# Streaming encoder step on one core: rows of v four steps behind rows of u, and another order of the first loads

## The reference, cut to what matters

```python
z = jnp.einsum('bld,de->ble', hn, w_in)            # hn = RMSNorm(x), projections of all tiles
...
def block(xb):                                     # 128 tokens
    qh = jnp.einsum('td,de->te', xb, w_q)...
    s = jnp.einsum('thcd,hcnd->thcn', qh, sub_keys)
    ...                                            # top 16 of 8 heads: eidx (128, 8, 16), gates g
    act = gelu(jnp.einsum('td,thkd->thk', xb, u_tab[eidx]))
    return jnp.einsum('thk,thkd->td', g * act, v_tab[eidx])
```

## Time and profile before

| | |
|---|---|
| median of 3 runs | 3998.46 us (3996.53 to 4018.43) |
| the profiled execution | 4045.73 us |
| its span, first to last instruction | 4044.0 us |
| busy: PE, DVE, POOL, ACT | 2780.5, 2535.5, 2261.6, 1054.3 us |
| moved by DMA | 1389.41 MB, mean 344 GB/s |
| queue of the indirect DMAs | 1215.35 MB, 79.9% of 16 engines' span |
| first rows of u issued | 312.87 us |
| first boundary (`turn_weights`) | 723.49 us |
| second boundary | 1110.24 us |
| last boundary | 3842.26 us |

### The profile page before, as it was taken

One profiled execution on the slowest core, in us unless ns is written; L12 is line 12 of the kernel. 1 busy time (PEld: TensorE's weight loads), 2 busy tenths in 40 slices (PEclk: granted clock), 3 DMA queues, 4 the chain that ended last, 5 costly groups with the idle time before them and its releaser, 6 DMA issues.

```text
span 4044.0 us, 48466 instructions
## 1 busy us (share of the span) xinstructions
PE 2780.5 (69%) x16300; PEld 1405.1 (35%) x16300; DVE 2535.5 (63%) x6869; ACT 1054.3 (26%) x2881; POOL 2261.6 (56%) x2365
## 2 busy tenths in 40 slices
PE   7999999677577747774777488658774674333365
PEld 6845644333234314441443144224331331000021
DVE  2445657775876678758776787687767556544400
ACT  3312212323232223222322323233322111110121
POOL 1102443666666666656666666665656666666665
PEclk9999999778677867776778687868875575555567
DMA  7645798999999999999999999999999999999998
GB/s 204 187 142 163 259 344 272 375 374 389 375 373 363 388 371 378 372 365 358 359 375 372 366 366 376 387 376 351 384 360 357 373 391 351 368 369 365 366 362 314
DMA packets 545781, 1389.41 MB, mean 344 GB/s; under 512 B 61289, under 2 KB 225313, under 8 KB 545537
## 3 DMA queue, kind: packets, MB, share of 16 engines
q0 software_dynamic: 335024, 1215.35, 79.9%
q1 hardware_dynamic: 198288, 161.34, 12.5%
q10 hardware_dynamic: 12224, 9.63, 0.9%
HBM read 1352.93 MB, written 33.04 MB: 343 GB/s over the span
## 4 chain that ended last, share of the span: by engine, by line
PE 16%; POOL 11%; DMA 11%; DVE 11%; issue 8%; another core or an unknown queue 5%; ACT 1%; DVEq 0%; ACTq 0%; POOLq 0%
POOL d_vb L1726 6%; DMA d_ub<-in_peer_u_dram,d_eid 5%; PE d_pY L1756 5%; POOL d_ub L1707 5%; DMA d_vb<-in_peer_v_dram,d_eidT 5%; DVE d_ub L1920 5%; PE d_pS L855 2%; PE r_pB L1456 2%; PE d_pS L941 1%; PE d_pS L921 1%; PE d_pS L880 1%; POOL d_ub L1726 1%; PE r_pB L1471 1%; PE d_pS L869 1%
## 5 line engine op out<-in xcount | busy, mean ns | idle before, releaser
L1920 DVE CUSTOM_DVE_ANT_0 d_ub<-d_ub,d_pX 128x1024 f32<-128x1024 f32 x1024 | 1242.5, 1218 | 645.9 <-DMA d_ub<-in_peer_u_dram,d_eid 515.9
L1707 POOL DMA_INDIRECT d_ub<-in_peer_u_dram,d_eid x1152 | 1135.6, 986 | 868.8 <-DVE d_hdot L1920 379.7
L1756 PE MATMUL d_pY<-d_vb,d_dg 128*32 128x256 f32 x8768 | 958.6, 515 | 851.2 <-DMA d_vb<-in_peer_v_dram,d_eidT 547.7
L1726 POOL DMA_INDIRECT d_vb<-in_peer_v_dram,d_eidT x1096 | 1043.2, 952 | 768.0 <-PE d_pY L1756 260.0
L1756 PEld LDWEIGHTS d_pY<-d_vb,d_dg 128*32 128x32 f32 x8768 | 256.2, 127 | 1459.1 <-issue 1273.7
L1795 ACT ACTIVATE d_dg<-c_late_sb,d_wgtT 128x32 f32<-128x32 f32 x1152 | 333.8, 314 | 1259.8 <-PE d_pY L1756 675.2
L707 PE MATMUL d_pX<-d_wq,d_vb 128*128 128x512 f32 (+3 forms) x1536 | 475.2, 462 | 17.8 <-DMA d_vb<-in_w_in_dram 9.7
L707 PEld LDWEIGHTS d_pX<-d_wq,d_vb 128*128 128x128 f32 x1536 | 271.9, 201 | 184.1 <-issue 117.5
L1456 PE MATMUL r_pB<-r_side,c_small_sb 128*128 128x128 f32 (+15 forms) x1152 | 175.7, 319 | 20.1 <-issue 14.0
L1920 DVE CUSTOM_DVE_ANT_0 d_ub<-d_ub,d_vb 128x1024 f32<-128x1024 f32 x128 | 155.2, 1220 | 49.6 <-DMA d_ub<-in_peer_u_dram,d_eid 46.4
L1456 PEld LDWEIGHTS r_pB<-r_side,c_small_sb 128*128 128x128 f32 x1152 | 174.7, 241 | 33.3 <-issue 23.7
(11 more groups left out here) (282 smaller groups left out, 3544.8 us busy)
## 6 DMA issues: line engine op xcount, KB each, us to landing
d_vb<-in_w_in_dram SPq DMA_DIRECT2D x68, 512.0 KB
d_ub<-in_peer_u_dram,d_eid POOLq DMA_INDIRECT x1152
d_vb<-in_peer_v_dram,d_eidT POOLq DMA_INDIRECT x1096
r_side<-in_cache_k_dram SPq DMA_DIRECT2D x16, 1024.0 KB
r_side<-in_cache_v_dram SPq DMA_DIRECT2D x16, 1024.0 KB
d_wo<-in_w_out_dram SPq DMA_DIRECT2D x6, 2048.0 KB, 9.4
d_wo<-in_peer_w_q_dram SPq DMA_DIRECT2D x4, 2048.0 KB, 8.9
scratch_h<-t_shared SPq DMA_DIRECT2D x9, 512.0 KB
```

The lines of the kernel that those rows point to most:

```text
L1707: pool.indirect_dma_start(out=ub[:, g % R, :], out_offset=None, in_=io["peer_u"][0], in_offset=off).then_inc(u_in[g % R], 16)
L1726: pool.indirect_dma_start(out=to, out_offset=None, in_=io["peer_v"][0], in_offset=off).then_inc(landed, 16)
L1756: m = nc.tensor.matmul(pY[q * QT:(q + 1) * QT, g % 2, :], dg[:, n % DG, :], rows[:, q * QD:(q + 1) * QD], start=k % QT == 0, stop=k % QT = ...
L1920: nc.vector.tensor_tensor_reduce(out=ub[:, g % R, :], in0=ub[:, g % R, :], in1=xflat if i else xn_of(0), scale=1.0, scalar=0.0, op0=ALU.mu ...
```

## The change

There are two parts.

**Rows of v four steps behind.** `LAG = 4`. The rows of v for expert `k` of tile `i - 1` are fetched and weighed in step `k + 4` of period `i`. `turn_weights` moves from step 0 to step 2, the copy of the weights and the first columns to step 3, `weigh` to step 1, the residuals, the last norm and the store by four steps. On ScalarE `copy_x` stands before `gelu`. TensorE's wait for `wT_done` moves from the start of a mixer to its first transposes.

**The beginning.** ScalarE issues x of the first tile and nothing else, and does one root of a constant before it waits. The eight small loads are issued by GpSimd, behind x of the second tile. The bias vector, the exponentials and the constants of the recurrence move from behind the first chunks to `pos[7]` to `pos[10]`, the eighth to the eleventh chunk, x of the third tile and the sub-keys behind the sixth segment (`p_acc` 6), `gfs` and `g2` behind x of the sixth tile, and the near blocks and keys by three chunks.

```diff
             load_x(1)
+            pool.dma_start(rb_, io["rel_bias"]).then_inc(c_t_in, 16)
...
+                pool.dma_start(lq[:, n, :], io[name].partition_broadcast(P)).then_inc(c_t_in, 16)
+            pool.wait_ge(p_acc, 6)
+            load_x(2)
...
             yield -320
-            act.dma_start(rb_, io["rel_bias"]).then_inc(c_t_in, 16)
...
+            act.dma_start(nx[:, 0, :], rows_of(io, "x", NORMS[0])).then_inc(p_first, 16)
             act.wait_ge(c_eps, 1)
-            act.wait_ge(p_first, 32)
+            nc.scalar.activation(nst[:, 3:4], eps[:], ACT.Sqrt)
+            act.wait_ge(p_first, 48)
...
-            at.append((-285, 3, exps, ()))
+            at.append((pos[8] + 0.9, 3, exps, ()))
...
+        LAG = 4
...
-                for i in range(NT + 1):
-                    for k in range(NEXP):
+                for i in range(NT + 2):
+                    for k in range(NEXP if i <= NT else LAG):
...
-                        if i:
-                            n = NEXP * (i - 1) + k
+                        n = NEXP * (i - 1) + k - LAG
+                        if n >= 0:
...
-                        if 1 <= i <= NT:
-                            if k == 0:
-                                turn_weights(i - 1)
-                            weigh_rows(i - 1, k)
+                        if 1 <= i <= NT and k == 2:
+                            turn_weights(i - 1)
+                        n = NEXP * (i - 1) + k - LAG
+                        if 0 <= n < NEXP * NT:
+                            weigh_rows(n // NEXP, n % NEXP)
...
-                        if 1 <= i and k == 0:
-                            finish(i)
+                        if 1 <= i <= NT and k == 1:
+                            weigh(i - 1, 1, CUT, NEXP)
...
+                        if i >= 2 and k == LAG + 1:
+                            residual(i - 2, 3)
```

More of the change, by code:

```diff
@@ L519, in proj_gpsimd @@
             pool.dma_start(hgn[:], io["hg_out_norm"].rearrange("a e -> e a"), allow_slow_non_contiguous=True).then_inc(c_k_in, 16)
+            pool.wait_ge(c_vec_done, 1)
+            pool.dma_start(sc["bv"], bv).then_inc(c_vec_out, 16)
+            pool.wait_ge(c_vec_out, 16)
+            for n in range(4):
+                pool.dma_start(back[:, n], shifted(n)).then_inc(c_back_in, 16)
+            for i in range(3, 6):
+                load_x(i)
+            pool.dma_start(cst["g2"][:], io["norm2"].partition_broadcast(P)).then_inc(c_in, 16)
+            pool.dma_start(cst["farb"][:], far_row.partition_broadcast(P)).then_inc(c_in, 16)
+            pool.dma_start(cst["late_sb"][:], late[:, P:LATE]).then_inc(c_in, 16)
             for q in range(4):
@@ L523, in proj_gpsimd @@
                                ).then_inc(c_in, 16)
[L524 to L533, removed]
+            for i in range(6, NT - 1):
                 load_x(i)
@@ L639, in proj_vector @@
             gain(0)
-            yield -286
+            yield norm_at[1] - 1.5
+            rstd(1)
+            yield norm_at[1] + 0.5
+            gain(1)
+            yield pos[7]
             dve.wait_ge(c_t_in, 16 * 8)
@@ L650, in proj_vector @@
             nc.vector.tensor_tensor(lbt[:, 2], lbl[:, 1], lbt[:, 0], ALU.subtract).then_inc(c_lb_diff, 1)
+            yield pos[9]
+            dve.wait_ge(c_vec_psum, 1)
+            nc.vector.tensor_copy(bv, pS[0:DH, 2, 0:BV]).then_inc(c_vec_done, 1)
+            yield pos[10]
             dve.wait_ge(c_exped, 1)
@@ L662, in proj_vector @@
             nc.vector.tensor_scalar(lbt[:, 5], lbt[:, 4], -1.0, 1.0, ALU.mult, ALU.add).then_inc(c_ready, 1)
-            dve.wait_ge(c_ready, 1)
-            dve.wait_ge(c_k_in, 16 * 4)
-            step(nc.vector.tensor_scalar(dan[:], dan[:], 1.0 - LAM_INIT, None, ALU.mult))
-            for i in range(1, NT):
+            for i in range(2, NT):
                 if i == NT - 1:
@@ L670, in proj_vector @@
                     dve.wait_ge(c_in, 16 * 7)
+                    dve.wait_ge(c_ready, 1)
+                    dve.wait_ge(c_k_in, 16 * 4)
+                    step(nc.vector.tensor_scalar(dan[:], dan[:], 1.0 - LAM_INIT, None, ALU.mult))
                     step(nc.vector.memset(offset[:], 0.0))
@@ L863, in turn @@
                         pe.wait_ge(o_done, U + u)
+                    if u == 0 and i >= 2:
+                        pe.wait_ge(wT_done, i - 1)
                     if u == 0 and i >= 3:
@@ L1860, in _ @@
                                     column(j, c)
-                            if k + AHEAD < NEXP:
-                                column(j, k + AHEAD)
+                            if 0 <= k - LAG and k - LAG + AHEAD < NEXP:
+                                column(j, k - LAG + AHEAD)
                             if k == 20:
```

61 lines of the change are left out of this document (27 added, 34 removed).

## The result

The changed kernel takes 4020.4 us (median of 22 runs, 4000.1 to 4032.78), the kernel before beside it 4006.23 us (22 runs, 3992.4 to 4024.11). The ratio is 1.0031, 95% interval 1.0021 to 1.0041: 0.31% slower, where 8 us less had been forecast, and outside the range of 3966 to 4003 us. The profiled execution of the changed kernel took 4024.15 us with a span of 4022.4 us. That is less than the profiled one of before (span 4044.0 us) although the medians stand the other way round. The profiled execution of before lies 40 us above its own median of 4006.23 us, more than the whole effect, so the totals of two single traces are no evidence here. Only stretches within them are, and best between traces from one chip.

What follows compares the result with a forecast made beforehand. PE was taken to bound the kernel before 715 us, the DMA engines from there to the last landing. Beginning -9.1, first boundary +1, later boundaries 0 gave -8 us: 3998.46 to 3990 us, range 3966 to 4003 us.

Steps and rivals of the forecast that it cites:

- the term of 5.7 us: At the start: earlier x and one table load fewer bring PE's first chunk 5.7 us forward (4.1 to 6.0).
- The beginning's terms: Before the gather: first chunk 5.7 us earlier, plus 3.4 us (0 to 8.6) less PE waiting for `w_in`.
- the two bursts: POOL's early loads split into two parts of 1.05 MB among one-tile chunks, priced at up to 5.2 us of waits.
- the forecast 304: End of the beginning: first rows of u issued at about 304 us instead of 312.87 us.
- The beginning as a whole: Everything gained at the start, first chunk and `w_in` waits together: 9.1 us, 4.1 to 14.6 us.
- Rival 3: The beginning pays less, `w_in` waits returning elsewhere: 5.7 us gained at most, 3993 to 4000 us; chance 0.15.
- 1 us of loss (0 to 5.2): First boundary: four v loads slip out of a stretch where the DMA engines have room, costing 1 us.
- a stall taken away there is worth nothing: 0 us ... not below zero but for the residual: Eight boundaries in the gather regime: shrinking DVE's 6.20 us idle gains 0 us, at most 50 us.
- Rival 4: At eight boundaries the residual wait grows from 6.20 past 11.7 us, losing 32 us: 4022 us; chance 0.10.

Runs made afterwards that it cites:

- kernel 14: The changed kernel with the lag of the v rows undone, so the beginning alone, timed again: 3824.29 us, ratio 0.9991 to the kernel before.
- 15: The changed kernel itself, unaltered, timed a third time: 3835.92 us, ratio 1.0037 to the kernel before.
- the fourth group: Four kernels timed on one chip, where the kernel before took 3825 us: the kernel before, beginning alone, changed kernel, and changed kernel with lag 1.
- Kernels 8 and 12: The changed kernel with every residual add of VectorE one step earlier (8: 4082.26 us, ratio 1.0102) or one step later (12: 3877.3 us, ratio 1.0140).
- kernel 18: The beginning alone, without a lag, with the last norm moved from step 5 to 9 and the stores from 8 to 12: 4009.74 us, ratio 1.0008.
- kernel 6: The changed kernel with a lag of five steps instead of four: 4041.1 us, ratio 1.0008 to the kernel before.

## Why the prediction was wrong

**Step by step.** The start: first chunk forecast at 11.8 us, measured 11.97 (11.88 in another trace); the term of 5.7 us held. Its lower bound was drawn a little wide (10.44 - 7.4 is 3.0 us, not 2.8). "The beginning's terms" for `w_in` did not hold: 3.4 us were forecast as gained, and PE's wait fell by 2.0 us, but a new wait of 6.7 us for ScalarE came at 54 us. I had priced the two bursts as DMA time between chunks. What stands beside each is an issue of SyncE that took 3 to 4 us, with the chunks and the transposed rows queued behind it. With both, the first row of u came at 310.0 us instead of the forecast 304. The 312.87 us of the trace of before make even this look like a gain of 2.9 us; on one chip it is 0.8 us for kernel 14 and nothing for 15 (310.08 us before, 309.25 and 310.35 us). The beginning as a whole is worth 0.8 to 5.5 us, not 9.1, with 4.1 us as the lower bound of the forecast. This is the first term that was mis-sized. Rival 3 describes it, and gives 3993 to 4000 us.

The first boundary, "1 us of loss (0 to 5.2)", is neither confirmed nor refuted: +1.6 or -1.6 us in one pair, by where the count begins, and kernel 3, which issues the four rows early, gained nothing.

**The step that failed** is "a stall taken away there is worth nothing: 0 us ... not below zero but for the residual". The first half was right as far as seen: DVE's idle time ahead of the residual shrank and bought nothing, where the DMA shares were 1.02 and 1.03. The second half was wrong, and it turned the sign: the lag alone costs 11 us, and 11.6 and 16.7 us beside the beginning alone. The lag doesn't only move the v rows and the residual. It moves the squares, the root, the last norm and the stores too, since all of them stand at `LAG` plus a constant, and I costed them at nothing without asking what stands at step 9. On the chip of the fourth group the steps around a boundary lost 2.2 us, 13 us for six. Steps 8 to 16, where the norm now stands and TensorE waits about 3 us instead of 1, lost 3.7 us, and the others gave some back.

Rival 4 had the sign. Its 4022 us beside 4020.4 is luck: it adds 24 us to a median of 3998.46, and the measured loss is 14 us on a median of 4006.23. Its condition didn't arise either, the wait ahead of the residual growing from 6.20 past 11.7 us; it shrank to 2.62 us. TensorE's wait for the residual did grow, from 46.3 to 71.9 us from 14 to 15, most of it at the boundary. There the residual stands at `LAG + 1`, one step further behind its rows than before, where it stood at step 0; the other three keep their distance. Kernels 8 and 12 show that such meetings cost about 1 us for each step of displacement. But lag 1 has the same extra step and stands at 0.9990, and steps 0 to 8 got shorter with lag 4 (21.8 beside 23.1 us), so the record speaks against this as the main cause. No kernel moved this residual alone.

**What stays open.** By the ratios moving the norm accounts for 5 to 10 us of the 11 to 17 us that lag 4 costs beside the beginning alone, and that with intervals that overlap. How it costs them is shown only as far as TensorE's wait. The rest of the loss has no cause shown. It may be the changed order of TensorE's products at steps 8 to 16, since lag 2, with the norm at step 7, loses as much there in its trace. Where the beginning loses its lead between the wide chunk (4.6 to 7.1 us earlier than before in pairs on one chip) and the first row of u (0.8 us at most) wasn't worked out. Nor is it explained why lags of 2 and 5 differ by 0.003 and 0.005 between chips. Lags of 6 and 8 were not tried.

No version beat the kernel before beyond its interval: the best three, beginning alone, lag 1 and lag 2, lie at 0.9986 to 0.9991, and lag 2 also at 1.0020.

## What to carry to other kernels

When a stream is shifted against a program written in steps, list everything that is placed relative to it, the small jobs too, and look up what already stands at the step where each will land: 1.85 us of VectorE work that moved from step 5 to step 9 lengthened a wait of TensorE there from about 1 to about 3 us. In a DMA-bound stretch an idle engine bought nothing when it was relieved, but each residual, a meeting of two engines at a fixed step, cost about 1 us when moved by one step either way, so such a place is the first to check after a shift. Rows left out at the beginning of a stream come back at its end, at some 1.6 us each here (6.4 us for four).

## What the runs showed of the hardware

- The same kernel (the one before) took 3825 us on two chips, 4007 to 4009 us on two, 4037 us on another. The difference is in the DMA-bound part: the changed kernel's first dot of tile 1 comes at 720.5 and 716.2 us on a slow and a fast chip, but from its last dot to the end it takes 207.2 and 189.9 us.
- The first 300 us differ by up to 9 us between kernels whose instructions are the same there, and mostly repeat within 2 us for each kernel across chips (the kernel before has 312.87 and 310.08 us). The first row of u is issued at 310.0, 310.4 and 310.4 us in the changed kernel, at 304.9 and 303.4 us with lag 2, at 310.8 and 310.0 us with lag 5, at 302.0 us in kernel 18 beside 308.0 and 309.3 us for the beginning alone. In the traces of lag 2 the wait for ScalarE at 50 us is 4.87 and 1.76 us long, where it is 6.70 and 6.45 us in the changed kernel. The times of SyncE's issues go along: between 20 and 60 us kernel 18 has one that took over 1.5 us (2.70 us), the slowest, kernel 6 with 310.8 us, has three (3.72, 1.74 and 4.39 us). Why the same order of instructions gives other times wasn't found. A few us of any ratio here can come from it, those of 18 and of lag 2 above all.
- The 32 transposes of one recurrence piece took 3.74 us at a granted clock of 1.00 (2.4 GHz) and 5.54 us at 0.66 in the mean, behind 3.11 us without work on TensorE, and 6.99 us at 0.50 (1.2 GHz) behind 0.98 us without.
